# Memory and first weights in one array, features on partitions, read in four quarters

## The reference

```
h       = rmsnorm(x, norm_pre);  cols = h @ w_in
mem_kv  = rmsnorm(mem, norm_mem) @ w_mem_kv      # mem: 256 x 1024, w_mem_kv: 1024 x 1024
mk, mv  = split(mem_kv)                          # keys and values of the memory branch, 4 heads of 128
s       = einsum(q, mk) * 128**-0.5;  p = softmax(s);  o = einsum(p, mv) * silu(z)
```

## Time and profile before

| what | value |
|---|---|
| median of three runs | 1400.03 us |
| profiled execution, its own time | 1400.76 us |
| its span | 1399.0 us |
| TensorE busy | 1387.1 us, 99% |
| VectorE, ScalarE busy | 909.2 us, 738.2 us |
| bytes moved | 239.13 MB, mean 171 GB/s |
| first product on weights | 9.54 us after the start of the span |

### The profile page before, as it was taken

The page is one execution under the profiler, slowest core; times in us unless marked ns, Lnnn a source line. Parts: engine busy times, 40 slices in busy tenths (PEclk is TensorE's granted clock), DMA queues, the critical chain, the costliest instruction groups (busy, mean ns, idle before and its releaser), DMA issues.

```text
span 1399.0 us, 21534 instructions
## 1 busy us (share of the span) xinstructions
PE 1387.1 (99%) x8348; PEld 1233.1 (88%) x8348; DVE 909.2 (65%) x1163; ACT 738.2 (53%) x909; POOL 75.0 (5%) x113
## 2 busy tenths in 40 slices
PE   9999999999999999999999999999999999999998
PEld 8989989988888888899888888888889999888886
DVE  5565788675566666666666666665667676665656
ACT  7566663344355444557555445544445458554444
POOL 2000010010020000020110000000000002200000
PEclk9999999999999999999999999999999999999999
DMA  8543431255535555461465555755555410555552
GB/s 323 199 171 121 157 145 61 91 200 202 187 134 203 203 182 189 171 206 66 162 261 190 200 181 179 247 203 181 180 184 197 156 36 1 214 193 184 201 185 90
DMA packets 34862, 239.13 MB, mean 171 GB/s; under 512 B 4010, under 2 KB 4154, under 8 KB 7152
## 3 DMA queue, kind: packets, MB, share of 16 engines
q1 hardware_dynamic: 33072, 231.46, 46.4%
q0 software_dynamic: 1296, 6.15, 1.2%
q10 hardware_dynamic: 432, 0.66, 0.1%
HBM read 236.11 MB, written 1.08 MB: 170 GB/s over the span
## 4 chain that ended last, share of the span: by engine, by line
PE 96%; ACT 2%; DVE 2%; issue 0%; POOL 0%; POOLq 0%; ACTq 0%; DVEq 0%
PE ps L736 22%; PE ps L706 16%; PE ps L708 15%; PE ps L707 15%; PE ps L744 12%; PE ps L1037 3%; PE ps L1011 2%; PE ps L1021 2%; PE ps L1361 1%; PE ps L2977 1%; PE ps L2985 1%; PE ps L645 1%; PE ps L2989 1%; PE ps L3156 1%; DVE low L412 1%; PE ps L827 1%
## 5 line engine op out<-in xcount | busy, mean ns | idle before, releaser
L412 DVE TENSOR_TENSOR low<-raw,high 128x2048 fp32r<-128x2048 f32 x211 | 480.6, 2279 | 229.5 <-ACT high L406 227.0
L406 ACT ACTIVATE high<-raw 128x2048 fp32r<-128x2048 f32 (+2 forms) x214 | 405.1, 1895 | 78.2 <-PE ps L708 73.2
L736 PE MATMUL ps<-nt,high 128*128 128x512 f32 x1344 | 320.1, 390 | 0.0
L736 PEld LDWEIGHTS ps<-nt,high 128*128 128x128 f32 x1344 | 249.0, 188 | 49.8
L744 PEld LDWEIGHTS ps<-nt,low 128*128 128x128 f32 x1344 | 167.5, 189 | 3.6
L744 PE MATMUL ps<-nt,low 128*128 128x256 f32 x1344 | 168.6, 283 | 0.0
L706 PE MATMUL ps<-high,hth 128*128 128x512 f32 x320 | 124.5, 389 | 0.0
L707 PE MATMUL ps<-low,hth 128*128 128x512 f32 x320 | 124.5, 389 | 0.0
L708 PE MATMUL ps<-high,htl 128*128 128x512 f32 x320 | 124.5, 389 | 0.0
L706 PE MATMUL ps<-nt,high 128*128 128x256 f32 x400 | 114.2, 286 | 0.0
L708 PE MATMUL ps<-nt,low 128*128 128x256 f32 x400 | 113.2, 283 | 0.0
(11 more groups left out here) (429 smaller groups left out, 2052.1 us busy)
## 6 DMA issues: line engine op xcount, KB each, us to landing
raw<-in_stream SPq DMA_DIRECT2D x214, 1024.0 KB, 4.8
late<-in_w POOLq DMA_DIRECT2D x1, 2048.0 KB, 9.4
scr<-bias_by_distance POOLq DMA_DIRECT2D x1, 2048.0 KB, 15.6
scr<-in_mem SPq DMA_DIRECT2D x2, 512.0 KB, 4.4
raw<-in_stream SPq DMA_DIRECT2D x4, 256.0 KB, 6.5
raw<-in_stream SPq DMA_DIRECT2D x2, 512.0 KB, 7.8
x<-in_x SPq DMA_DIRECT2D x1, 1024.0 KB, 8.4
scr<-scr SPq DMA_DIRECT2D x8, 128.0 KB, 2.3
```

The source lines that it names most:

```text
L406: nc.scalar.activation(high_of(t, slice(0, n)), raw[t % SLOTS][:, 0:n], ACT.Copy).then_inc(w_high, 1)
L412: nc.vector.tensor_tensor(low_of(t, slice(0, n)), raw[t % SLOTS][:, 0:n], high_of(t, slice(0, n)).bitcast(F32), ALU.subtract).then_inc(w_l ...
L736: last = nc.tensor.matmul(r3(bank, 2), w[:, k, P * j:P * j + P], nt[:, :, k, :], start=first and k == 0, stop=not first and k == KC - 1, s ...
```

## The change

The host lays out one more array, `first`: for each partition four quarters of 1024 numbers, each with two chunks of 128 features of mem, transposed (2 x 256 tokens), followed by a quarter of tile 0. SyncE brings it in four transfers of 512 KB into a part of `late` that is not in use yet (`opening`), in place of the two halves of mem and the four quarters of tile 0. The sixteen transposes of mem and the entry "mem" of the turns go away; ScalarE and VectorE make the two halves of `nt_m` from `opening` directly. mem by token is still read, in one transfer, for the squares of its norm. It and x are now asked for behind tile 2 and ahead of tile 3 without a wait. The squares of mem move on ScalarE to behind the read of mk0's bank, all at once. ScalarE makes one small copy at the start. TensorE runs eight idle products in place of four and three, and waits for the identity only before the memory's root.

```diff
+        "first": np.concatenate([a["mem"][0].T.reshape(KC, P, S).transpose(1, 0, 2).reshape(P, 4, 2 * S),
+                                 stream[0].reshape(P, 4, TW // 4)], axis=2), "row": row, "con": con,
...
+        opening = r3(late[:, 0:KC * S + TW], PARTS)
...
-            sp.dma_start(norm_src["mem"][:, 0, :], A["mem"][:, 0, :]).then_inc(mem_here[0], 16)
-            sp.dma_start(norm_src["mem"][:, 1, :], A["mem"][:, 1, :]).then_inc(mem_here[1], 16)
-            for b in range(4):
-                c = slice(512 * b, 512 * b + 512)
-                sp.dma_start(raw[0][:, c], A["stream"][0, :, c]).then_inc(raw_here[0] if b == 3 else first_here[b], 16)
+            for b in range(PARTS):
+                sp.dma_start(opening[:, b, :], A["first"][:, b, :]).then_inc(raw_here[0] if b == PARTS - 1 else first_here[b], 16)
...
                 sp.dma_start(raw[t][:], A["stream"][t]).then_inc(raw_here[t], 16)
+            sp.dma_start(norm_src["mem"], A["mem"]).then_inc(mem_here, 16)
+            sp.dma_start(x[:, :, :], A["x"]).then_inc(x_here, 16)
             for t in range(SLOTS, 2 * SLOTS):
                 sp.wait_ge(w_low, t - SLOTS + 1)
                 sp.dma_start(raw[t % SLOTS][:], A["stream"][t]).then_inc(raw_here[t % SLOTS], 16)
                 if t == SLOTS:
-                    sp.dma_start(x[:, :, :], A["x"]).then_inc(x_here, 16)
...
-            act_norm(act, "mem", (0,))
+            zeroed_here(act, "first_ones")
+            nc.scalar.activation(mark_col, one_col, ACT.Copy)
             act.wait_ge(ident_here, 16)
...
+            for b in range(PARTS):
+                act.wait_ge(raw_here[0] if b == PARTS - 1 else first_here[b], 16)
+                for k in range(2):
+                    last = nc.scalar.activation(NTM[0][:, 2 * b + k, :], opening[:, b, S * k:S * k + S], ACT.Copy,
+                                                scale=vcol("mem", 2 * b + k))
+                last.then_inc(mem_high, 1)
+                nc.scalar.activation(high_of(0, slice(512 * b, 512 * b + 512)), opening[:, b, 2 * S:], ACT.Copy)\
+                    .then_inc(w_high if b == PARTS - 1 else first_high, 1)
...
-            act_norm(act, "mem", (1,))
             for name, dst in (("mk0", xm["k"][:, 0:512]), ("mk1", xm["k"][:, 512:1024])):
                 act_step(act, name)
                 bank_read(name, nc.scalar.activation(dst, read_bank(act, name)[:, :], ACT.Copy))
+                if name == "mk0":
+                    act_norm(act, "mem")
...
+                dve.wait_ge(mem_high, b + 1)
+                for k in range(2 * b, 2 * b + 2):
+                    src = opening[:, b, S * (k % 2):S * (k % 2) + S]
+                    last = nc.vector.scalar_tensor_tensor(out=NTM[1][:, k, :], in0=src, scalar=vcol("mem", k),
+                                                          in1=NTM[0][:, k, :].bitcast(F32), op0=ALU.mult,
+                                                          op1=ALU.subtract)
+                last.then_inc(mem_low, 1)
...
-            pe_idle_products(sw["k"][:, 0:P], sw["k"][:, 256:512], 4, ps[6][:, 0:S])
-            pe.wait_ge(ident_here, 16)
-            for t in range(TT):
-                pe.wait_ge(mem_here[t], 16)
...
-            pe_idle_products(sw["k"][:, 0:P], sw["k"][:, 256:512], 3, ps[6][:, 0:S])
+            pe_idle_products(sw["k"][:, 0:P], sw["k"][:, 256:512], 8, ps[6][:, 0:S])
...
-                    pe.wait_ge(turn_low, turn_at["mem"] + k // 2 + 1)
+                    pe.wait_ge(mem_low, k // 2 + 1)
...
             pe_pair_tile(pe, "mv0", 0, NTM)
+            pe.wait_ge(ident_here, 16)
             pe.wait_ge(row_here, 32)
             pe_late_root(pe, "mem")
```

More of the change, by code:

```diff
@@ L252, in lay_out @@
     arrays = {
-        "stream": stream, "x": tok(a["x"]), "mem": tok(a["mem"]), "row": row, "con": con,
+        "stream": stream, "x": tok(a["x"]), "mem": tok(a["mem"]),
+        "first": np.concatenate([a["mem"][0].T.reshape(KC, P, S).transpose(1, 0, 2).reshape(P, 4, 2 * S),
+                                 stream[0].reshape(P, 4, TW // 4)], axis=2), "row": row, "con": con,
         "level": level, "hot": hot,
@@ L454, in build @@
         TURNS = {
-            "mem": (xs, 8, "mem") + NTM, "pre": (xs, 8, "pre", nth, ntl),
+            "pre": (xs, 8, "pre", nth, ntl),
             "ym": (as3(xm["y"], TT), 4, None, yth[:, 0], ytl[:, 0]),
@@ L541, in build @@
         SPREAD = ["mem", "f0", "f1", "f2", "mx1", "f3"]
+        opening = r3(late[:, 0:KC * S + TW], PARTS)
+        mem_high, mem_low = s_("mem_high"), s_("mem_low")
         norm_src = {"mem": scr[:, 0:TT * D].rearrange("p (t c) -> p t c", t=TT)}
@@ L559, in act_norm @@
                 if name == "mem":
-                    act.wait_ge(mem_here[t], 16)
+                    act.wait_ge(mem_here, 16)
                 if name == "pre":
@@ L1203, in build @@
         first_high, first_low = s_("first_high"), s_("first_low")
-        mem_here, ident_here, x_here, row_here = [s_("mem_here0"), s_("mem_here1")], s_("ident_here"), s_("x_here"), \
+        mem_here, ident_here, x_here, row_here = s_("mem_here"), s_("ident_here"), s_("x_here"), \
             s_("row_here")
@@ L2288, in _ @@
                 c = slice(512 * b, 512 * b + 512)
-                dve_turn(dve, "mem", slice(b, b + 1))
+                dve.wait_ge(mem_high, b + 1)
[5 more added lines that the diff above has]
+                last.then_inc(mem_low, 1)
                 if b == 3:
@@ L2293, in _ @@
                     dve.wait_ge(first_high, b + 1)
-                nc.vector.tensor_tensor(low_of(0, c), raw[0][:, c], high_of(0, c).bitcast(F32), ALU.subtract)\
+                nc.vector.tensor_tensor(low_of(0, c), opening[:, b, 2 * S:], high_of(0, c).bitcast(F32), ALU.subtract)\
                     .then_inc(w_low if b == 3 else first_low, 1)
```

## The result

| | before | after |
|---|---|---|
| median of 22 runs each | 1401.3 us (1399.89 to 1402.25) | 1403.18 us (1402.06 to 1406.09) |
| ratio, 95% interval | | 1.0017 (1.0011 to 1.0022), +2.4 us |
| profiled execution, its own time | 1400.76 us | 1402.06 us |
| its span | 1399.0 us | 1400.3 us |
| bytes moved | 239.13 MB | 240.18 MB |

The forecast was 1400.8 us, range 1398.6 to 1402.7. The time is above it: the changed kernel is slower, by little (0.17%), and the interval of the ratio does not hold 1. The two medians lie 1.9 us apart, the ratio says 2.4, the two profiled executions 1.3.

The account below looks back on a forecast made before the run. TensorE's queue was taken to bound the kernel: the 2.2 us gained at the start would be lost waiting for x behind late tile 3, net +0.75 us on the 1400.03 median, giving 1400.8 us, range 1398.6 to 1402.7.

Parts of the forecast that it names:

- The first product: TensorE's first weight product in the opening would start at 7.3 us instead of 9.54.
- the clock rose: TensorE's rise from 1.2 to 2.4 GHz during the opening's idle products was put near 6 us.
- the gain at the start: In the opening, TensorE would start its weight products 2.2 us earlier; nothing of this would be left before x.
- Rival (a): Tile 3 lands in time and the early start is kept: 1398.7 to 1400.0 us, chance 0.33.
- Rival (c): Idle products stay slow to 9.3 us, so TensorE starts no earlier: 1400.8 us again, chance counted within the forecast's 0.52.
- the chain of x: Before mv1, from the start of x's squares to the second scaled x: 4.32 us, giving 28.8 us.
- the 22.1 taken: Tile 3's landing in the opening, put at 22.1 us from its bytes plus a queue lag.
- 0.9 was taken: Before mv1, the second eight transposes would end 0.9 us after the second scaled x, at 29.7 us.
- the forecast +0.75: mv1 and everything behind it would come 0.75 us later, at 29.7 instead of 28.96 us.
- the hole before the transposes: TensorE, through mv0's first half and root at 24.95, would wait about 2.3 us for the first scaled x.
- Rival (b): TensorE's clock drops to 1.2 GHz in the hole before x, costing 2.1 us: 1402.9 us, chance 0.12.

Follow-up runs that it names:

- x_first: Changed kernel with ScalarE reading mk1's bank and squaring x before splitting tile 3, and VectorE's scaled x before tile 3's low half: 1401.10 us, ratio 0.9998.
- reordered: Changed kernel asking for x, tiles 3 and 4, then mem, with four engines' orders fitted to the landings: 1399.97 us, ratio 0.9992.
- no_mem_rows: Changed kernel without the transfer of mem by token; its norm's squares read other numbers: 1401.01 us, ratio 0.9996.
- bank_first: Changed kernel with ScalarE reading mk1's bank before it splits tile 3: 1404.11 us, ratio 1.0021.
- low3_behind: Changed kernel with VectorE's low half of tile 3 behind the scaled x: 1403.62 us, ratio 1.0022.
- hole_filled: Changed kernel with five idle products between the two halves of mv0's first tile: 1403.07 us, ratio 1.0014.
- after_again: The changed kernel itself, unedited, timed again beside other runs: 1403.79 us, ratio 1.0019.
- mem_twice: Changed kernel asking for mem by token twice, ScalarE waiting for both copies: 1406.51 us, ratio 1.0040.
- tile3_first: Changed kernel with mem by token and x asked for behind tile 3, ScalarE's order kept: 1403.69 us, ratio 1.0017.
- reordered_2: The kernel reordered, with ScalarE reading mk1's bank before it splits tile 3: 1399.87 us, ratio 0.9993.

## Why the prediction was wrong

**What held.** TensorE has hardly any idle time, and a change counts by when it gets through the opening. By the traces that is the start of xmq0 rather than of mv1: 36.16 in after, 33.77 in x_first and 33.11 in reordered against 34.27 before, with ratios of 1.0017, 0.9998 and 0.9992. The first product came at 7.72 (forecast 7.3). ScalarE's first scaling began at 5.15 and not at 4.8, released by the landing of the gains (asked for at 0.74, 4.38 us) and not by quarter 0; that is most of the 0.4. The idle products end there too: read one by one, the first twelve start 0.43 us apart and the last four 0.26, so the clock rose nearer 7 than 6 us. The queue moved 418 GB/s; the Trainium skill ("DMA: Bandwidth & Descriptors", section Bandwidth) has 358 for the HBM side and 425 for a core that is alone, and the trace agrees with the second. The additional 1 MB cost tile 3 2.35 us (no_mem_rows), and the gain at the start was lost in front of x, in the chain and at the places named: tile 3, the squares, the scaled x, a wait between the two groups of eight transposes. The rest behind mv1 ran as before. Rival (a), that tile 3 would come in time, is out: it came at 22.49. Rival (c), that TensorE would not start earlier, is out: it started 1.8 us earlier.

**The step that failed** is the price of the chain of x: "the second tile of scaled x is ready after 26.81 - 22.49 = 4.32 us". It measured 4.89 (24.79 to 29.68). I took the duration from before, where VectorE was idle until the roots came, and moved it to a place where it runs the low half of tile 3; GpSimd's operation took until that was done, 0.77 us instead of 0.19. bank_first shows the same from the other side (1.25 us, ending with the low half again), low3_behind takes the low half away and has 0.19 again. The Trainium skill ("SBUF — State Buffer", section Who interferes with whom) has a rule for it: a VectorE instruction with two inputs in SBUF contends with a GpSimd instruction that reads SBUF, over a pair of ports that is locked and not shared out. The trace agrees, and shows that here the wait lasts to the end: 26.78 against VectorE's 26.72. The size of this miss is 0.57 us.

The trace of before had it already, in lines that the prediction does not set side by side. GpSimd's operation at 15.18 took 0.70 us and ended at 15.88; VectorE's second low half of tile 1, with two inputs in SBUF, ended at 15.83:

```profile
13.46 2.37 DVE L2302 TENSOR_TENSOR low<-raw,high 128x1024 fp32r<-128x1024 f32 x2
```

**Terms that were mis-sized.** Tile 3 landed 0.4 us later than the 22.1 taken; the bytes give 20.6 by the rates of after, so the lag was 1.9 us, that of the row of x, and I had taken 1.6. The squares then began at 24.79 instead of 24.45. The second eight transposes ended 1.1 us after the scaled x (29.68 to 30.82), where 0.9 was taken: 0.2. Together 0.34 + 0.57 + 0.2 = 1.1 us, which is what lies between the forecast +0.75 and the measured +1.86 at mv1. The largest of the three is the chain of x.

**The base.** I put the 0.75 us on the median of three runs, 1400.03. Over 22 runs before has 1401.3. Its executions lie in two groups, around 1400.1 and around 1401.9, and three out of three had fallen in the lower one. Of the 2.4 us by which 1400.8 was missed, 1.3 is this, more than the mechanism's 1.1, and it was bad luck in the sample and no fault in the chain. Either of the two alone would have left the time below 1402.7. What parts the groups is likely the half-pace stretch near 614 us: it is in the profiled executions of five kernels (x_first, no_mem_rows, reordered, hole_filled, after_again), costs about 1.5 us there, and is missing in before's and after's own profiles. The mean granted clocks of before's 80 runs beside the experiments fit it: the 40 faster ones have 0.998 or 0.999, of the 40 slower ones 33 have 0.997 and 7 have 0.998. That the stretch parts the runs of before was not traced.

**The hole in the wrong place.** The prediction let TensorE run through mv0's first tile to 24.95 and put the hole before the transposes. It overlooked a wait that was already in the code and covered: the second half of that tile needs mk1's bank, read behind tile 3's split. In before the read began at 21.33, long before the product that needs it:

```profile
23.88 0.39 PE L706 MATMUL ps<-high,nt_m 128*128 128x512 f32 x1
```

bank_first shows that the place of the hole is worth nothing.

**Rival (b), the clock falls in the hole,** was given 0.12. It is neither out nor the explanation. In after's profiled execution the products behind the hole keep their 0.23 us. In low3_behind's they don't, nor in mem_twice's. Of the runs of the five kernels that leave TensorE without work for 2.0 to 2.8 us (after, after_again, bank_first, tile3_first, low3_behind), 11 of 64 had a mean granted clock of 0.996 or less (mem_twice apart: 2 of 5); of those without it, 0 of 80 of before and 0 of 55 of x_first, no_mem_rows, hole_filled, reordered and reordered_2. In after these are the four highest times: 1403.99, 1404.73, 1405.48 and 1406.09 us, one to three us above the median. So the hole likely costs a second time in some runs. How often is not shown: none of the 11 was traced, and low3_behind's profiled execution, where the fall is traced, has a mean of 0.998 and is not among them. Where the hole is filled with idle products no run was above 1404.05, and four of ten of after_again beside it were. For the median this is worth some tenths (hole_filled 1403.07 beside after_again 1403.79), within the intervals of both.

**What stays open:** why the clock falls behind some holes and not behind others of nearly the same length, and why the stretch near 614 us comes in some runs, with TensorE at work before and through it. No kernel was made for either.

## What to carry to other kernels

A transfer that is asked for earlier goes ahead of all that is asked for later: count the bytes that now stand in front of the next weight tile, add the time from the last byte to the landing that the nearest row shows (1.9 us here, in a full queue), and put the consuming engines' orders in the order of the landings, or nothing is gained. A duration taken from the trace holds only with the neighbours it had there: look at what the engine beside it will be running at the new time. When an early start is followed by a hole, every wait behind it that was covered, such as a bank's read, has to be worked out anew.

## What the runs showed of the hardware

- A GpSimd operation on 128x1 took 0.19 us beside an idle VectorE. It took 0.77 (after) and 1.25 (bank_first) beside a VectorE operation with two inputs in SBUF, and ended 0.05 us behind it each time. Beside VectorE's scaled x, with one input in SBUF, it took 0.75 (after, 27.50) and 0.62 (x_first, 22.38), and ended 0.05 us behind that too.
- TensorE after 2.0 to 2.8 us without work went on at full pace (0.23 us from one product of 512 columns to the next) in after, after_again, bank_first and tile3_first, and at half pace (0.43) in low3_behind; after 5.2 us, in mem_twice, at half pace. Twelve products then took 1.5 us longer. In the middle of the kernel, with TensorE busy throughout, there are some 3 us at a granted clock of 0.50 in the traces of five kernels.
- As the queue goes over to the weight stream (6 to 7.25 us), four transfers of 512 KB in runs of 4 KB go ahead of it with no slow stretch (416 GB/s); with four of 256 KB in runs of 2 KB it had 162.
